# Expert-row combine: slots 0 to 3 fetched into four buffers and added at least two expert blocks later, slot 5 added by TensorE

## The chip, the cores and the metric

The kernel runs on one core of one Trainium2 chip. The metric is the device time of one execution in microseconds (us), lower is better. A core has TensorE (PE, matmuls into PSUM banks), VectorE (DVE), ScalarE (ACT), GpSimd (POOL) and SyncE (SP); SP, ACT and POOL also issue DMAs, which all run on the same 16 DMA engines.

## The reference

A transformer block of one kind (attention and a state-space branch, cross attention, then a mixture of experts) followed by one of another kind. The change touches the mixture of experts, its layer norm and the start of the second block:

```python
scores = sigmoid(x @ w_router)                 # 512 tokens, 64 experts, d = 1024
top_idx = 8 best experts of the 4 best groups of 8
w = scores[top_idx]; w = w / sum(w) * 2.5
for expert e: out_e = swiglu(x[tokens of e], w_exp_gu[e], w_exp_down[e])
routed[t] = sum over the 8 chosen experts of w * out_e[row of t]
ff = routed + swiglu(x, w_sh_gu, w_sh_down)    # the shared expert
x = layer_norm(2 ** 0.25 * x + ff, ln3_g, ln3_b)
h = rmsnorm(x); z = h @ w_in                   # the second block begins
```

Everything is float32.

## The kernel before, in words

The kernel is written as one program for each engine, with semaphores between them; nothing is scheduled automatically, so the order of each program is the order of the work.

**Expert blocks.** `e_block(u, b)` handles expert e = 4u + b on every engine, 64 of them. On PE a block turns the hidden rows of expert e-1 (L1240, `turn_hidden`), turns the gathered tokens of expert e+1 (L1233, `turn_rows`, which waits for that expert's gather), does the gate-up product of expert e (L1271) with the down product of expert e-2 woven in (L1279, L1289). PE waits for `ht_ready`, which DVE gives when it has copied the turned hidden rows (L2340, `hidden_turned`). ACT and DVE evacuate the results into `ye`, and ACT stores 96 rows per expert in `y_rows` (`y_send`, L1732; L1777 for the last two). POOL gathers the 96 token rows of expert e+1 or so from `x_rows` (L2716). SP loads 2 MB of gate-up and 1 MB of down weights per expert (L823, L826) into four slots: gate-up in `ring[:, 0:4096]`, `ring[:, 4096:8192]`, `slab1`, `slab2`.

**Slots.** The eight choices of a token are its slots 0 to 7, in the order of the experts' numbers. For slot k and token tile t (four tiles of 128 tokens) POOL gathers 128 rows of 4 KB from `y_rows` with an indirect DMA (`slot_rows(k, t)`, L2726), and the row is scaled by its weight and added to `acc`. Slot k can be fetched when expert 56 + k is stored (`slot_stored(k)`), since its row cannot belong to a later one. Slots 0 to 4 and 6 share the one buffer `work[:, 0:4096]`: tile t of slot k+1 is fetched when tile t of slot k has been added (semaphore `combined`). Slot 5 has `slab1`, slot 7 has `slab2`. DVE adds slots 0 to 6 (`combine(k, t)`, the L1926 instructions on `work,s5x,slab`, 128x1024): slots 0, 1, 2, 3 inside blocks 60, 61, 62, 63 between `y_rest` and the copy of the down results (L2384), slot 4 around the last two down products, then slots 5 and 6. PE adds slot 7 by a product of the diagonal matrix of its weights with the rows (`last_slot`, L1347), on top of the shared expert's down product (L1340) in the banks `sd`.

**After the slots.** For each tile DVE adds the `sd` banks and takes the moments (`slots_added`), POOL computes the root, DVE and ACT normalise, PE turns the result (`hT2`, L949) and begins the second block's first product, `uv` (L940). Its weights come as panels of `stream` in the ring buffer (L811); SP starts these loads once 24 adds are done (`combined` 24) and needs nothing else, since slots do not use the ring.

Of the kernel before, what the change touches and what calls it, by code (L numbers as in the profile page):

```python
# [27 lines left out]
ACT = mybir.ActivationFunctionType  # L28
# [496 lines left out]
def build(nc, a, out, scratch):  # L525

    plan = Plan(psum_order(), 8)
    with ExitStack() as ctx:
# [3 lines left out]
        def sem(name):  # L532
            return ctx.enter_context(nc.semaphore(name))
# [3 lines left out]
        def tile(name, i):  # L537
            return bank[plan.where[name, i]]
# [135 lines left out]
        diag = [work[:, 4096 + t * P:4096 + (t + 1) * P] for t in range(NT)]  # L674
        w_main, w_over, yrow_f = s5x[:, 3464:3496], s5x[:, 3496:3528], s5x[:, 3528:3560]
# [84 lines left out]
        ov = {n: sem("ov_" + n) for n in ("gather", "w", "store", "xtr", "xe", "gu", "silu", "hid", "ht", "htr", "dn", "yact", "ydve", "idx", "ygot", "added")}  # L760
        ygot = {k: [sem(f"ygot{k}_{t}") for t in range(NT)] for k in (0, 5, 7)}
        for k in (1, 2, 3, 4, 6):
            ygot[k] = ygot[0]
        diag_ready, acc_scaled = sem("diag_ready"), sem("acc_scaled")
# [30 lines left out]
        def _(sp):  # L795
# [102 lines left out]

            sp.wait_ge(combined, 24)
            for n in range(N1, len(PANELS)):  # L900
# [10 lines left out]
        def _(pe):  # L911
# [430 lines left out]

            def last_slot(t):
                pe.wait_ge(ygot[7][t], 16)
                pe.wait_ge(diag_ready, t + 1)
                for half in range(2):
                    mm = nc.tensor.matmul(tile("sd", 2 * t + half)[:, :], diag[t], yslot[7][t][:, half * 512:half * 512 + 512],  # L1347
                                          start=False, stop=True)
                    close(mm, "sd", 2 * t + half)
# [168 lines left out]
        def _(act):  # L1518
# [259 lines left out]
            act.wait_ge(w_ready, 1)  # L1778
            for t in range(NT):
                nc.scalar.activation(diag[t], ident, ACT.Copy, scale=w_main[:, 28 + t:29 + t]).then_inc(diag_ready, 1)  # L1780
            act.wait_ge(route_ctrl, 3)
# [26 lines left out]
            act.wait_ge(combined, 28)  # L1808
            act.dma_start(wsT, a["gmlp_ws"]).then_inc(in_ln, 16)
# [92 lines left out]
        def _(dve):  # L1902
# [452 lines left out]
            def combine(k, t):  # L2355
                dve.wait_ge(acc_scaled, t + 1)
                dve.wait_ge(ygot[k][t], 16 * {5: 1, 6: 6}.get(k, k + 1))
# [44 lines left out]
            for b in range(2):  # L2402
                combine(4, 2 * b)
                dve.wait_ge(y_stored[b], 16 * (NE // 2 - 1))
                y_full(b, 5 - 5 * b, dnf_full, b + 1, yf_dve)
                combine(4, 2 * b + 1)
            dve.wait_ge(combined, added[0])
# [42 lines left out]

            for t in range(NT):
                combine(5, t)
            dve.wait_ge(in_ln, 96)
# [178 lines left out]
        def _(pool):  # L2632
# [89 lines left out]

            def slot_rows(k, t, buf_free=None):
                if buf_free is not None:
                    pool.wait_ge(combined, buf_free)
                pool.indirect_dma_start(yslot[k][t], None, scratch["y"][0:CAP * PITCH, :],  # L2726
                                        bass.IndirectOffsetOnAxis(ap=yrow_i[:, 4 * k + t:4 * k + t + 1].bitcast(U32), axis=0),
                                        bounds_check=CAP * PITCH - 1, oob_is_err=False).then_inc(ygot[k][t], 16)

# [5 lines left out]
            for e in range(NE):  # L2735
# [7 lines left out]
                gather(e)  # L2743
            for k in range(1, 5):
                slot_stored(k)
                for t in range(NT):
                    slot_rows(k, t, 4 * (k - 1) + t + 1)
            n_ov = pool.value_load(ctrl_i[0:1, NOV:NOV + 1], min_val=0, max_val=NOV)
            with pool.If(n_ov > 0):
                pool.wait_ge(xtr_full, NE)  # L2750
                nc.gpsimd.tensor_copy(tiny[:, 4:5], minus_half[:, 0:1]).then_inc(ov["idx"], 1)
                with pool.Fori(0, NOV) as o:
                    with pool.If(n_ov > o):
                        pool.wait_ge(idx_ov, 16 * o + 16)
# [16 lines left out]
                pool.wait_ge(ov["added"], 4 * TOPK)  # L2771

            slot_stored(5)
            pool.wait_ge(gu_full, 3 * NE)
            for t in range(NT):
                slot_rows(5, t)
            pool.wait_ge(combined, 20)
# [72 lines left out]
```

## Time and profile before

| what | value |
|---|---|
| median of 3 runs | 2170.53 us (2170.22 to 2173.47) |
| the profiled execution | 2177.02 us, its span 2175.2 us |
| PE, DVE, ACT, POOL busy | 1979.7, 779.9, 465.7, 335.5 us |
| mean granted clock of PE | 0.972 of 2.4 GHz |
| expert blocks and slots | about 670 to 1366 us of the span |

The busy times are sums over the whole span; the times of instructions below are counted from the span's start. "Idle before" in a timeline row stands in square brackets with what ended it. A matmul of float32 counts as two instructions in the trace.

### The profile page before, as it was taken

The numbers are of one execution on the slowest core, as the hardware profiler recorded it, in microseconds if no ns is written. First come the engines' busy times: TensorE is split into PE (matmuls) and PEld (weight loads), VectorE is DVE, ScalarE is ACT, GpSimd is POOL, SyncE is SP. The second block draws the span as 40 slices with busy tenths as digits, with TensorE's granted clock in tenths as the row PEclk, the third lists the DMA queues.
The fourth block names the chain that finished last, engine by engine and source line by source line (L and its number), as shares of the span: only waits on it lengthen the run. The fifth ranks groups of instructions, "written<-read, shape, count | busy, mean of one in ns | idle before, by whom it ended". The sixth has DMA issues, their size and how long they took to land.

```text
span 2175.2 us, 25449 instructions
## 1 busy us (share of the span) xinstructions
PE 1979.7 (91%) x9890; PEld 909.8 (42%) x9890; DVE 779.9 (36%) x1577; ACT 465.7 (21%) x1023; POOL 335.5 (15%) x295
## 2 busy tenths in 40 slices
PE   7887999999997999998989857699989899999997
PEld 3334434445543344433333322345745444444443
DVE  5998781214266233323232326501375200000012
ACT  2234431110310233333333311210263000000000
POOL 0653260000025211011000014200032000000000
PEclk9898999999999999999999988799999999999999
DMA  5129934213235999999999986512310222222210
GB/s 227 48 65 205 213 96 163 77 49 119 97 139 188 342 398 402 402 398 387 387 380 389 387 337 224 206 68 86 117 40 1 77 77 77 77 77 77 69 38 29
DMA packets 74723, 393.59 MB, mean 181 GB/s; under 512 B 12194, under 2 KB 12450, under 8 KB 57760
## 3 DMA queue, kind: packets, MB, share of 16 engines
q1 hardware_dynamic: 45216, 300.95, 36.7%
q10 hardware_dynamic: 16592, 58.01, 9.6%
q0 software_dynamic: 12848, 33.74, 4.4%
q8 instruction: 42, 0.69, 0.1%
q14 instruction: 25, 0.20, 0.0%
HBM read 371.51 MB, written 55.09 MB: 196 GB/s over the span
## 4 chain that ended last, share of the span: by engine, by line
PE 69%; DMA 15%; DVE 8%; issue 5%; POOL 2%; ACT 1%; another core or an unknown queue 0%; SPq 0%; POOLq 0%; DVEq 0%; ACTq 0%
PE bank L940 42%; DMA slab<-w_exp_down 13%; PE bank L1271 12%; PE bank L1492 6%; PE bank L949 2%; DVE slab L1926 1%; PE bank L1289 1%; DVE work L1920 1%; DVE s5x L1923 1%; DVE slab L1923 1%; PE bank L1002 1%; POOL slot_table L2705 1%; DVE slab L1920 1%; PE bank L1079 1%; PE bank L1233 1%
## 5 line engine op out<-in xcount | busy, mean ns | idle before, releaser
L940 PE MATMUL bank<-slab,ring 128*128 128x512 f32 (+1 forms) x1488 | 631.1, 585 | 13.1 <-DMA ring<-stream 11.4
L940 PEld LDWEIGHTS bank<-slab,ring 128*128 128x128 f32 x1488 | 281.8, 190 | 357.3 <-issue 354.7
L1271 PE MATMUL bank<-ring,slab 128*32 128x512 f32 x1536 | 230.2, 602 | 41.0 <-issue 24.1
L1271 PE MATMUL bank<-slab 128*32 128x512 f32 x1536 | 230.5, 599 | 29.7 <-DMA ring<-w_exp_down 17.4
L940 PE MATMUL bank<-ring,slab 128*128 128x512 f32 (+1 forms) x608 | 251.1, 573 | 3.6 <-DVE slab L1923 1.8
L1279 PE MATMUL bank<-ring,slab 128*32 128x512 f32 x512 | 228.8, 599 | 0.0
L1923 DVE TENSOR_TENSOR slab<-bank,slab 96x256 f32<-96x256 f32 (+2 forms) x120 | 64.7, 540 | 438.5 <-PE bank L940 295.0
L2384 DVE COPY slab<-bank 32x512 f32<-32x512 f32 x124 | 80.9, 688 | 392.9 <-PE bank L1279 392.8
L1279 PE MATMUL bank<-slab 128*32 128x512 f32 x480 | 213.2, 597 | 0.0
L940 PEld LDWEIGHTS bank<-ring,slab 128*128 128x128 f32 x608 | 114.9, 190 | 136.3 <-issue 128.6
L2641 POOL TENSOR_TENSOR small<-small 128x1 f32<-128x1 f32 (+2 forms) x30 | 26.6, 889 | 907.1 <-DVE small L1920 907.1
L1492 PE MATMUL bank<-ring,slab 128*128 128x512 f32 x352 | 151.3, 592 | 0.8 <-DVE slab L1923 0.8
L1271 PEld LDWEIGHTS bank<-ring,slab 128*32 128x32 f32 x1536 | 72.7, 111 | 173.2 <-issue 173.2
L1271 PEld LDWEIGHTS bank<-slab 128*32 128x32 f32 x1536 | 70.3, 110 | 163.9 <-issue 154.6
L2716 POOL DMA_INDIRECT slab<-x_rows,s5x x64 | 61.5, 961 | 499.3 <-PE bank L1233 479.5
L1492 PEld LDWEIGHTS bank<-ring,slab 128*128 128x128 f32 x352 | 66.8, 190 | 85.3 <-issue 83.7
L1752 ACT ACTIVATE slab<-bank 32x512 f32<-32x512 f32 x124 | 66.6, 584 | 117.5 <-PE bank L1279 108.9
L1708 ACT ACTIVATE slab<-bank 128x384 f32<-128x384 f32 x128 | 55.8, 488 | 161.8 <-DVE slab L2351 144.8
L1898 ACT ACTIVATE slab<-bank 128x512 f32<-128x512 f32 x22 | 13.1, 597 | 281.8 <-PE bank L940 281.8
L949 PE MATMUL bank<-const_sb,work 128*128 128x128 f32 x304 | 48.1, 292 | 20.3 <-DVE work L1920 14.9
L1233 PE MATMUL bank<-const_sb,slab 96*128 96x96 f32 x512 | 53.9, 249 | 11.7 <-DMA slab<-x_rows,s5x 10.6
L1525 ACT ACTIVATE slab<-bank 128x512 f32<-128x512 f32 (+2 forms) x40 | 22.7, 574 | 180.0 <-PE bank L940 170.2
(281 smaller groups left out, 2095.7 us busy)
## 6 DMA issues: line engine op xcount, KB each, us to landing
ring<-stream SPq DMA_DIRECT2D x171, 512.0 KB, 3.5
slab<-w_exp_gu SPq DMA_DIRECT2D x32, 2048.0 KB
ring<-w_exp_gu SPq DMA_DIRECT2D x32, 2048.0 KB
ring<-w_exp_down SPq DMA_DIRECT2D x32, 1024.0 KB
slab<-w_exp_down SPq DMA_DIRECT2D x32, 1024.0 KB
y_rows<-zeros ACTq DMA_DIRECT2D x1, 24960.0 KB, 130.7
y_rows<-slab ACTq DMA_DIRECT2D x64, 384.0 KB
gb<-rows ACTq DMA_DIRECT2D x5, 512.0 KB, 5.3
```

The costliest lines, as they stand in the source:

```text
L940: mm = nc.tensor.matmul(dst, lhs[k], rhs[k], start=(k == 0), stop=(k == len(lhs) - 1))
L949: mm = nc.tensor.transpose(tile(name, i)[0:parts, j * P:(j + 1) * P], x, ident)
L1233: mm = nc.tensor.transpose(bank[j][:, k * CAP:(k + 1) * CAP], xg[b][0:CAP, (4 * j + k) * P:(4 * j + k + 1) * P], ident[0:CAP, 0:CAP])
L1271: mm = nc.tensor.matmul(g_bank[32 * g:32 * g + 32, :], x[:, k, 32 * g:32 * g + 32], w[:, 512 * k:512 * k + 512], start=(k == 0), stop=(k = ...
L1279: mm = nc.tensor.matmul(bank[2 + 3 * t + half][96:128, :], h[:, c * CAP + 32 * t:c * CAP + 32 * t + 32], d[:, c * D + 512 * half:c * D + 5 ...
L1492: return nc.tensor.matmul(tile("fd", 4 * half + t)[:, :], actf[k][:, t * P:(t + 1) * P], panel("fd", 11 * half + k // 2)[:, (k % 2) * 512: ...
L1708: i = nc.scalar.activation(xe[b][:, 4 * j:4 * j + 4, :], bank[j][:, 0:4 * CAP].rearrange("p (k n) -> p k n", n=CAP), ACT.Copy)
L1752: i = nc.scalar.activation(ye[b % 2][0:32, 512 * half:512 * half + 512], bank[2 + half][96:128, :], ACT.Copy)
L1920: return nc.vector.tensor_scalar(out_, in_, s1, s2, op0, op1)
L1923: return nc.vector.tensor_tensor(out_, x, y, op)
L2384: i = nc.vector.tensor_copy(ye[b % 2][32:64, 512 * half:512 * half + 512], bank[5 + half][96:128, :])
L2716: pool.indirect_dma_start(xg[e % 2][0:CAP, :], None, scratch["x2"], bass.IndirectOffsetOnAxis(ap=slot_tok[:, e:e + 1].bitcast(U32), axis=0 ...
```

## The change

Slots get homes: slot 0 and 4 in `work`, 1 and 7 in `ring[:, 0:4096]`, 2 in `ring[:, 4096:8192]`, 3 and 6 in `slab1`, 5 in `slab2`. POOL fetches slots 1 to 3 when the gate-up product that uses that buffer is over, no longer when the slot before has been added. DVE adds slot 0 in block 62, slot 1 in block 63, slot 2 around the last down products, slots 3 and 4 after them, then slot 6. Slot 5 is added by PE with a second set of diagonal matrices. A slot in `work`, `ring_hi` or `slab2` has one semaphore for its four tiles together. The panels of the second block are loaded when the last slot product is over.

```diff
-        yslot = {k: [x[:, t * D:(t + 1) * D] for t in range(NT)] for k, x in ((0, work), (5, slab1), (7, slab2))}
-        for k in (1, 2, 3, 4, 6):
-            yslot[k] = yslot[0]
+        SLOT_HOME = {0: "work", 1: "ring_lo", 2: "ring_hi", 3: "slab1", 4: "work", 5: "slab2", 6: "slab1", 7: "ring_lo"}
...
+        home_got = {h: [sem(f"{h}_got{t}") for t in range(NT if h in ("slab1", "ring_lo") else 1)] for h in homes}
+        def ygot(k, t):
+            g = home_got[SLOT_HOME[k]]
+            return g[t % len(g)], 16 * nth_use[k] * (NT // len(g))
...
-            sp.wait_ge(combined, 24)
+            sp.wait_ge(combined, 12)
+            sp.wait_ge(psum_full, plan.full("sd", 7))
             for n in range(N1, len(PANELS)):
                 load_panel(n)
...
+            def add_slot(k, t):
+                pe.wait_ge(*ygot(k, t))
+                pe.wait_ge(diag_ready, t + 1 + 4 * (k == 7))
                 for half in range(2):
+                    mm = nc.tensor.matmul(tile("sd", 2 * t + half)[:, :], diag[k][t], yslot[k][t][:, half * 512:half * 512 + 512],
+                                          start=False, stop=(k == 7))
...
             for t in range(3):
                 shared_down(t)
-            last_slot(0)
+            add_slot(5, 0)
+            add_slot(5, 1)
+            add_slot(7, 0)
             shared_down(3)
-            for t in range(1, NT):
-                last_slot(t)
+            add_slot(5, 2)
+            add_slot(7, 1)
+            add_slot(5, 3)
+            add_slot(7, 2)
+            add_slot(7, 3)
...
             for b in range(4):
-                e_block(NE // 4 - 1, b, first=1, slot_=b)
+                e_block(NE // 4 - 1, b, first=1, slot_=b - 2 if b >= 2 else None)
...
-                combine(4, 2 * b)
+                combine(2, 2 * b)
...
-            for t in range(NT):
-                combine(5, t)
+            for k in (3, 4):
+                for t in range(NT):
+                    combine(k, t)
...
-            for k in range(1, 5):
+            for k in range(1, 4):
                 slot_stored(k)
+                pool.wait_ge(gu_full, 3 * (NE - 4 + k))
                 for t in range(NT):
-                    slot_rows(k, t, 4 * (k - 1) + t + 1)
+                    slot_rows(k, t)
...
+            slot_stored(4)
+            pool.wait_ge(combined, 4)
+            for t in range(NT):
+                slot_rows(4, t)
             slot_stored(5)
             pool.wait_ge(gu_full, 3 * NE)
             for t in range(NT):
                 slot_rows(5, t)
-            pool.wait_ge(combined, 20)
             slot_stored(6)
             for t in range(NT):
+                pool.wait_ge(combined, 13 + t)
                 slot_rows(6, t)
                 if t == 0:
                     slot_stored(7)
```

On DVE, in the unrolled blocks 60 to 63, this is the order before from the hidden rows of block 60 on; the four SCALAR_TENSOR_TENSOR are `combine`.

```order
L2340 COPY slab<-bank 128x96 x2
L1923 TENSOR_TENSOR slab<-bank,slab 96x256
L2350 COPY slab<-bank 32x256
L2351 COPY slab<-bank 32x256
L1926 SCALAR_TENSOR_TENSOR slab<-work,s5x,slab 128x1024 x4
L2384 COPY slab<-bank 32x512 x2
L2340 COPY slab<-bank 128x96 x2
```

And this is the order now, from the last operation of block 61 to the first add of slot 1.

```order
L2397 COPY slab<-bank 32x512 x2
L2353 COPY slab<-bank 128x96 x2
L1936 TENSOR_TENSOR slab<-bank,slab 96x256
L2363 COPY slab<-bank 32x256
L2364 COPY slab<-bank 32x256
L1939 SCALAR_TENSOR_TENSOR slab<-work,s5x,slab 128x1024 x4
L2397 COPY slab<-bank 32x512 x2
L2353 COPY slab<-bank 128x96 x2
L1936 TENSOR_TENSOR slab<-bank,slab 96x256
L2363 COPY slab<-bank 32x256
L2364 COPY slab<-bank 32x256
L1939 SCALAR_TENSOR_TENSOR slab<-ring,s5x,slab 128x1024 x4
```

In blocks 60 and 61 no add stands any more between the copies that PE waits for; the first four stand in block 62.

On POOL, the gathers at the end of the expert blocks were in this order, the x_rows gather being that of expert 63.

```order
L2726 DMA work<-y_rows,yrow_i 128x1024 x4
L2716 DMA slab<-x_rows,s5x 96x1024
L2726 DMA work<-y_rows,yrow_i 128x1024 x16
```

Now they are in this order.

```order
L2738 DMA work<-y_rows,yrow_i 128x1024 x4
L2730 DMA slab<-x_rows,s5x 96x1024
L2738 DMA ring<-y_rows,yrow_i 128x1024 x8
L2738 DMA slab<-y_rows,yrow_i 128x1024 x4
```

The four gathers of slot 0 are still ahead of the gather of expert 63, and slots 1 to 3 go elsewhere behind it.

On PE, after the last down product, the shared product and the slot product stood so.

```order
L1340 MATMUL bank<-work,s5x 128x512 x12
L1347 MATMUL bank<-slab,work 128x512 x2
L1340 MATMUL bank<-work,s5x 128x512 x4
L1347 MATMUL bank<-slab,work 128x512 x6
```

Now slot 5 (the rows in `slab`) stands among them.

```order
L1346 MATMUL bank<-work,s5x 128x512 x12
L1353 MATMUL bank<-slab,s5x 128x512 x4
L1353 MATMUL bank<-ring,work 128x512 x2
L1346 MATMUL bank<-work,s5x 128x512 x4
L1353 MATMUL bank<-slab,s5x 128x512 x2
L1353 MATMUL bank<-ring,work 128x512 x2
L1353 MATMUL bank<-slab,s5x 128x512 x2
L1353 MATMUL bank<-ring,work 128x512 x4
```

Four matmuls of slot 5 are ahead of the first of slot 7, and eight in all are new.

## Rows read from the trace of the kernel before

**Rows 1.** Windows: busy us of each engine, PE's granted clock, DMA share, GB/s.

```profile
1200.00:1250.00 50.00, 44.68 (x452) 18.87 (x450) 15.06 (x38) 15.37 (x36) 4.78 (x5) 1.00 1.01 387
1280.00:1290.00 10.00, 0.00 (x0) 0.00 (x0) 1.81 (x2) 0.37 (x1) 1.00 (x1) 0.70 0.94 363
1290.00:1300.00 10.00, 0.00 (x0) 0.00 (x0) 4.11 (x5) 0.00 (x0) 2.01 (x3) 0.50 0.65 224
```

**Rows 2.** Timeline of PE: start us, us, instructions [idle before, what ended it].

```profile
1270.02 0.63 PE L1271 MATMUL bank<-ring,slab 128*32 128x512 f32 x3 [0.60 <-DMA slab<-w_exp_down]
...
1279.07 0.24 PE L1233 MATMUL bank<-const_sb,slab 96*128 96x96 f32 x1 [0.22 <-DMA slab<-w_exp_down]
1301.28 1.07 PE L1271 MATMUL bank<-ring,slab 128*32 128x512 f32 x3 [21.96 <-issue]
...
1310.91 0.82 PE L1233 MATMUL bank<-const_sb,slab 96*128 96x96 f32 x8
1312.04 0.63 PE L1271 MATMUL bank<-slab 128*32 128x512 f32 x3 [0.30 <-issue]
...
1319.91 0.39 PE L1240 MATMUL bank<-const_sb,slab 96*128 96x96 f32 x2
1326.24 1.07 PE L1271 MATMUL bank<-slab 128*32 128x512 f32 x3 [5.95 <-issue]
...
1336.82 0.39 PE L1240 MATMUL bank<-const_sb,slab 96*128 96x96 f32 x2
```

**Rows 3.** Timeline of DVE, blocks 60 and 61.

```profile
1283.40 1.28 DVE L1926 SCALAR_TENSOR_TENSOR slab<-work,s5x,slab 128x1024 f32<-128x1024 f32 x1 [12.72 <-DMA work<-y_rows,yrow_i]
...
1297.90 1.28 DVE L1926 SCALAR_TENSOR_TENSOR slab<-work,s5x,slab 128x1024 f32<-128x1024 f32 x1 [3.88 <-DMA work<-y_rows,yrow_i]
...
1300.55 0.42 DVE L2340 COPY slab<-bank 128x96 f32<-128x96 f32 x2
```

**Rows 4.** Timeline of POOL: gathers of slots (L2726) and of expert 63 (L2716).

```profile
1271.86 1.02 POOL L2726 DMA_INDIRECT work<-y_rows,yrow_i  x1 [10.70 <-DMA y_rows<-slab]
...
1277.08 0.98 POOL L2716 DMA_INDIRECT slab<-x_rows,s5x  x1 [0.30 <-issue]
1285.56 1.00 POOL L2726 DMA_INDIRECT work<-y_rows,yrow_i  x1 [7.50 <-DVE slab L1926]
...
1356.19 1.61 POOL L2726 DMA_INDIRECT slab<-y_rows,yrow_i  x1 [1.21 <-DMA y_rows<-slab]
...
1365.27 0.99 POOL L2726 DMA_INDIRECT slab<-y_rows,yrow_i  x1 [0.30 <-issue]
```

**Rows 5.** Timeline of ACT's queue: the last store of expert rows.

```profile
1350.42 0.32 ACTq L1777 DMA_DIRECT2D y_rows<-slab  x1
```

**Rows 6.** Timeline of PE from the shared product to the second block.

```profile
1351.76 12.26 PE L1340 MATMUL bank<-work,s5x 128*128 128x512 f32 x24 [2.23 <-issue]
1363.87 1.88 PE L1347 MATMUL bank<-slab,work 128*128 128x512 f32 x4
1365.58 3.60 PE L1340 MATMUL bank<-work,s5x 128*128 128x512 f32 x8
...
1380.64 3.78 PE L1347 MATMUL bank<-slab,work 128*128 128x512 f32 x4 [1.91 <-DMA slab<-y_rows,yrow_i]
1395.43 5.93 PE L949 MATMUL bank<-const_sb,slab 128*128 128x128 f32 x32 [11.00 <-ACT slab L1801]
```

**Rows 7.** Timeline of DVE: the first add of slot 5, then the tiles' sums.

```profile
1354.45 2.48 DVE L1926 SCALAR_TENSOR_TENSOR slab<-slab,s5x 128x1024 f32<-128x1024 f32 x2 [2.93 <-issue]
...
1364.99 1.48 DVE L1923 TENSOR_TENSOR slab<-bank,slab 128x512 f32<-128x512 f32 x2 [3.48 <-PE bank L1347]
...
1370.80 1.48 DVE L1923 TENSOR_TENSOR slab<-bank,slab 128x512 f32<-128x512 f32 x2 [0.19 <-PE bank L1347]
```

**Rows 8.** DMA issues from 1345 to 1420 us: KB each, median us to landing.

```profile
ring<-stream SPq DMA_DIRECT2D x12, 512.0 KB, 15.7
...
slab<-y_rows,yrow_i POOLq DMA_INDIRECT x8, 7.1
```

More of the change, by code:

```diff
@@ L670, in build @@
         dn_w = [ring[:, 8192:10240], ring[:, 10240:12288], slab3[:, 0:2048], slab3[:, 2048:4096]]
-        yslot = {k: [x[:, t * D:(t + 1) * D] for t in range(NT)] for k, x in ((0, work), (5, slab1), (7, slab2))}
-        for k in (1, 2, 3, 4, 6):
-            yslot[k] = yslot[0]
-        diag = [work[:, 4096 + t * P:4096 + (t + 1) * P] for t in range(NT)]
+        SLOT_HOME = {0: "work", 1: "ring_lo", 2: "ring_hi", 3: "slab1", 4: "work", 5: "slab2", 6: "slab1", 7: "ring_lo"}
+        homes = {"work": work[:, 0:4096], "ring_lo": ring[:, 0:4096], "ring_hi": ring[:, 4096:8192], "slab1": slab1[:, :], "slab2": slab2[:, :]}
+        yslot = {k: [homes[h][:, t * D:(t + 1) * D] for t in range(NT)] for k, h in SLOT_HOME.items()}
+        nth_use = {k: sum(SLOT_HOME[j] == h for j in range(k + 1)) for k, h in SLOT_HOME.items()}
+        diag = {5: [s5x[:, 2048 + t * P:2048 + (t + 1) * P] for t in range(NT)],
+                7: [work[:, 4096 + t * P:4096 + (t + 1) * P] for t in range(NT)]}
         w_main, w_over, yrow_f = s5x[:, 3464:3496], s5x[:, 3496:3528], s5x[:, 3528:3560]
@@ L760, in build @@
         ov = {n: sem("ov_" + n) for n in ("gather", "w", "store", "xtr", "xe", "gu", "silu", "hid", "ht", "htr", "dn", "yact", "ydve", "idx", "ygot", "added")}
-        ygot = {k: [sem(f"ygot{k}_{t}") for t in range(NT)] for k in (0, 5, 7)}
-        for k in (1, 2, 3, 4, 6):
-            ygot[k] = ygot[0]
+        home_got = {h: [sem(f"{h}_got{t}") for t in range(NT if h in ("slab1", "ring_lo") else 1)] for h in homes}
+        def ygot(k, t):
+            g = home_got[SLOT_HOME[k]]
+            return g[t % len(g)], 16 * nth_use[k] * (NT // len(g))
         diag_ready, acc_scaled = sem("diag_ready"), sem("acc_scaled")
@@ L1341, in shared_down @@
                                          sd_w[:, k * D + half * 512:k * D + half * 512 + 512], start=(k == 0), stop=False)
-            def last_slot(t):
-                pe.wait_ge(ygot[7][t], 16)
-                pe.wait_ge(diag_ready, t + 1)
+            def add_slot(k, t):
+                pe.wait_ge(*ygot(k, t))
+                pe.wait_ge(diag_ready, t + 1 + 4 * (k == 7))
                 for half in range(2):
-                    mm = nc.tensor.matmul(tile("sd", 2 * t + half)[:, :], diag[t], yslot[7][t][:, half * 512:half * 512 + 512],
-                                          start=False, stop=True)
-                    close(mm, "sd", 2 * t + half)
+                    mm = nc.tensor.matmul(tile("sd", 2 * t + half)[:, :], diag[k][t], yslot[k][t][:, half * 512:half * 512 + 512],
+                                          start=False, stop=(k == 7))
+                    if k == 7:
+                        close(mm, "sd", 2 * t + half)
             for t in range(3):
                 shared_down(t)
-            last_slot(0)
+            add_slot(5, 0)
+            add_slot(5, 1)
+            add_slot(7, 0)
             shared_down(3)
-            for t in range(1, NT):
-                last_slot(t)
+            add_slot(5, 2)
[3 more added lines that the diff above has]
+            add_slot(7, 3)
             for c in range(KD):
@@ L1778, in _ @@
             act.wait_ge(w_ready, 1)
-            for t in range(NT):
-                nc.scalar.activation(diag[t], ident, ACT.Copy, scale=w_main[:, 28 + t:29 + t]).then_inc(diag_ready, 1)
+            for k in (5, 7):
+                for t in range(NT):
+                    nc.scalar.activation(diag[k][t], ident, ACT.Copy, scale=w_main[:, 4 * k + t:4 * k + t + 1]).then_inc(diag_ready, 1)
             act.wait_ge(route_ctrl, 3)
@@ L1807, in _ @@
                 scaled(t)
-            act.wait_ge(combined, 28)
+            act.wait_ge(combined, 24)
             act.dma_start(wsT, a["gmlp_ws"]).then_inc(in_ln, 16)
@@ L2356, in combine @@
                 dve.wait_ge(acc_scaled, t + 1)
-                dve.wait_ge(ygot[k][t], 16 * {5: 1, 6: 6}.get(k, k + 1))
+                dve.wait_ge(*ygot(k, t))
                 if t in last_add:
@@ L2402, in _ @@
             for b in range(2):
-                combine(4, 2 * b)
+                combine(2, 2 * b)
                 dve.wait_ge(y_stored[b], 16 * (NE // 2 - 1))
                 y_full(b, 5 - 5 * b, dnf_full, b + 1, yf_dve)
-                combine(4, 2 * b + 1)
+                combine(2, 2 * b + 1)
             dve.wait_ge(combined, added[0])
@@ L2449, in ln3_scale @@
                 stt(tm(x3, t), tm(x3, t), r, gb[:, D:2 * D], ALU.mult, ALU.add).then_inc(x3_ready, 1)
-            for t in range(NT):
-                combine(5, t)
+            for k in (3, 4):
+                for t in range(NT):
+                    combine(k, t)
             dve.wait_ge(in_ln, 96)
@@ L2721, in _, with slot_rows @@
             pool.wait_ge(x2_stored, 16 * NT)
-            def slot_rows(k, t, buf_free=None):
-                if buf_free is not None:
-                    pool.wait_ge(combined, buf_free)
+            def slot_rows(k, t):
                 pool.indirect_dma_start(yslot[k][t], None, scratch["y"][0:CAP * PITCH, :],
                                         bass.IndirectOffsetOnAxis(ap=yrow_i[:, 4 * k + t:4 * k + t + 1].bitcast(U32), axis=0),
-                                        bounds_check=CAP * PITCH - 1, oob_is_err=False).then_inc(ygot[k][t], 16)
+                                        bounds_check=CAP * PITCH - 1, oob_is_err=False).then_inc(ygot(k, t)[0], 16)
             def slot_stored(k):
@@ L2764, in _ @@
                     pool.wait_ge(y_stored[b], 16 * NE // 2)
-                pool.wait_ge(combined, 20)
+                pool.wait_ge(combined, 12)
                 for j in range(4 * TOPK):
@@ L2771, in _ @@
                 pool.wait_ge(ov["added"], 4 * TOPK)
+            slot_stored(4)
+            pool.wait_ge(combined, 4)
+            for t in range(NT):
+                slot_rows(4, t)
             slot_stored(5)
@@ L2776, in _ @@
                 slot_rows(5, t)
-            pool.wait_ge(combined, 20)
             slot_stored(6)
             for t in range(NT):
+                pool.wait_ge(combined, 13 + t)
                 slot_rows(6, t)
```

## The prediction

> **What bounds the kernel now.** I read the windows of ten microseconds first. In the expert blocks (1200 to 1250) PE is busy 44.7 of 50 us and the DMA engines are full at 387 GB/s; then come twenty microseconds in which PE does nothing [rows 1]. The timeline of PE gives the edges: it has turned the tokens for block 61's successor at 1279.31 (1279.07 + 0.24), and the gate-up product of block 61 starts at 1301.28, after 21.96 us idle [rows 2]. The trace calls the releaser "issue", which names nobody. DVE's timeline names it: the copy of the turned hidden rows that PE waits for is at 1300.55, and ahead of it stand the four adds of slot 0, the first after 12.72 us of waiting for its gather, the last at 1297.90 after another wait for one [rows 3]. So the adds, in the program between copies that PE needs, pass DVE's wait for a DMA on to PE. A second such stop is 5.95 us ahead of block 63 [rows 2]. What is slow is the gather: POOL issued it at 1271.86 [rows 4] and the data came 11 to 26 us later, because the weights filled the DMA engines [rows 1]. After the blocks PE, DVE and POOL share a chain through the tiles: PE's slot product, DVE's sums, the root, the turn `hT2` at 1395.43 [rows 6, 7]. Whatever moves that turn moves the end: nothing behind it is edited.
>
> **The change part by part.**
>
> *Blocks 60 and 61.* DVE holds no add in them now, so block 61 starts on PE as block 60 did: 0.6 us after the turning [rows 2], at 1279.9 in place of 1301.3. From a block's first product to the end of its turning of tokens takes 9.3 us (1270.02 to 1279.31); less the turning (0.8, the row at 1310.91) block 61 is through at 1288.4.
>
> *A new wait in block 62.* There PE turns the tokens of expert 63, whose gather POOL issues at 1277.08, behind the four gathers of slot 0 [rows 4], exactly as before. When it lands no row says. The last of slot 0, next ahead in the same queue, landed by 1297.90 [rows 3]; before the change PE turned these rows at 1310.91 without a wait [rows 2]. The four gathers of slot 0 (0.52 MB each) came through 14.5 us apart in all (1283.40 to 1297.90), 4.8 a piece; the 0.39 MB of this one cost 3.6 more at that rate, or 1.0 at the 387 GB/s of the full engines: 1298.9 to 1301.5. I take 1300.5. Two stores of expert rows, held back by the stop before, are now made in this stretch: 0.79 MB at 387 GB/s, 2.0 us. So the tokens are there at 1302.5, PE is idle for some 14 us, and the product of block 62 starts a turning later (1.1, from 1310.91 to 1312.04) at 1303.6, not 1312.04: 8.4 us gained. The earlier fetches of slots 1 and 2 are behind it in POOL's queue and cost it nothing as long as that order holds; that is the weak point, taken up below. Behind PE at this wait stand the products of blocks 62 and 63, and the two copies ACT and DVE make from them; DVE adds slot 0 in that time, which hides its 5.1 us (4 x 1.28).
>
> *The rest of blocks 62 and 63.* PE comes out of an idle stretch at 1.2 GHz (granted clock 0.50 in the windows' row 1290 to 1300 [rows 1]). Block 62, which started warm, takes 8.26 us from 1312.04 to the end of the turned hidden rows at 1320.30; block 63, after 5.95 idle, 10.97; block 61, after 21.96 idle, 9.6 to its end at 1310.9. A cold start so costs 1.4 to 2.7, I take 2.1. Before, from block 62's start: 8.26 + 5.95 + 10.97 = 25.2. Now: 8.26 + 2.1, then 1.3 for the copies between two blocks (between 0.6, the gap at 1270, and 2), then 8.26: 19.9. Gained 5.3, in all 13.7 at the end of block 63. Slot 1, added by DVE in block 63, was fetched over thirty microseconds earlier. The down products behind, and with them the last store (1350.42 [rows 5]), move by the same 13.7, to 1336.7.
>
> *POOL.* The first gather of slot 7 followed that last store by 5.8 us (1356.19 [rows 4]), so it can go at 1342.5. Slot 6 now waits for the adds of slot 3. DVE starts those where it started slot 5: 1354.45 - 13.7 = 1340.8 [rows 7], the first is done at 1342.1, and POOL issues 0.9 later, as it did at 1285.56 after the add at 1283.40 [rows 3, 4]: 1343.0. The order is 6, 7, 6, 7, so slot 7's first is issued at 1344.3, and eight gathers at 1.3 us put the last at 1352.1. With a median of 7.1 us to landing [rows 8] slot 7 is there from 1351.4 to 1359.2.
>
> *PE's tail.* The shared product starts at 1351.76 - 13.7 = 1338.1 and takes 12.1 [rows 6], to 1350.2. Then two tiles of slot 5 come first. A tile is 4 instructions, 1.71 us by 1363.87 to 1365.58: 3.4, to 1353.6. That is where slot 7's first tile may start; it landed at 1351.4, so its fetch is hidden with 2.2 us to spare. DVE adds the bank 1.1 after (1363.87 to 1364.99 [rows 6, 7]): 1354.7 against 1364.99, 10.3 gained. For the second tile PE does slot 7 (1.7), the shared product (3.4; 3.60 with overlap), slot 5 (1.7): 1360.4, and DVE can add at 1361.5 against 1370.80: 9.3 gained. From there DVE sets the pace, 6 to 7 us a tile, and PE needs 3.4 a tile. So of 13.7 us 4.4 are given back to the eight added matmuls, and 9.3 reach `hT2`.
>
> *DVE's tail.* Four adds leave (slot 5), eight come (slots 3, 4). They end at 1340.8 + 8 x 1.26 = 1350.9, slot 6's first at 1352.2, 2.5 ahead of the 1354.7 at which PE lets it go on: hidden, and 2.5 us of cover is all there is.
>
> *The panels.* They were issued from 1360 on, and are now issued from 1368 (PE's last slot product: 1360.4 + 1.7 x 4 + wait). `uv` needs eight of them 7 us after `hT2`, so at 1393. 4.2 MB at 387 GB/s take 10.9: hidden by 14 us, and even with the 15.7 us to landing of a crowded queue [rows 8] the eighth issue at 1374 arrives at 1390. For slots 6 and 7 it is a gain: PE's waits for slot 7 (1.91 at 1380.64 [rows 6]) had the panels beside them. I count none of it, as DVE sets the pace.
>
> *A rule.* The POOL gather at 1356.19 took 1.61 in place of 0.99 and ended 0.87 after DVE's adds did (1354.45 + 2.48 [rows 4, 7]). The Trainium skill, "SBUF — State Buffer", section "SBUF: two separate sides", says that DVE with two SBUF inputs and a GpSimd operation that reads SBUF exclude each other for a whole instruction; that row agrees. By the row a gather pays for one add, and since an add (1.26) is as long as an issue, the sum above stands. If POOL never gets in between adds that follow without a gap, it is the second rival.
>
> **The rivals.**
>
> 1. *As worked out*: 9.3 us faster, 2161.2 (5 to 13 us with the bounds: landing 1298.9 to 1304, cold start 1.4 to 2.7, gap 0.6 to 2). 54 in 100.
> 2. *POOL locked out by eight adds in a row.* Slot 6's first gather, due at 1343.0, then ends only when the adds do, 1350.9 + 0.9 = 1351.8; slot 7's first is issued at 1352.1 and lands at 1359.2, 5.6 later than PE could use it. The second tile is worth 3.7: 2167. For it: the 1.61. Against: that gather paid for what was left of adds already running, no more. 13 in 100.
> 3. *The gather of expert 63 is not held up*: the engines finish its parts out of order with slot 0's. PE then is not cold, and block 62 starts at 1289.5; another 14 + 2 us, 2145. Against it speaks that the engines are full up to 1290 (363 GB/s [rows 1]). Half of it is as likely: 2153. 8 in 100 together.
> 4. *The engines are the bound, and the change only fills them earlier.* Slots 1 and 2 (4.2 MB), the last 1 MB of weights and two stores (0.8 MB) are put into the stretch in which expert 63's tokens are awaited. If they share the engines with it instead of standing behind, 6.0 MB at 387 GB/s delay it by 15.5 us, at the 224 GB/s of the window 1290 to 1300 by 27. Block 62 then starts 13.5 to 25 later than I say, and the kernel is 4 to 16 us slower: 2175 to 2186. It is slower than before from a delay of 11 us on. For it: the slow gather of slot 0 under weights shows that queues share. Against: slot 0's four came in turn. 12 in 100.
> 5. *No change*: the stop moves whole from block 61 to 62 (tokens at 1308) and the tail takes the rest; 2168 to 2172. 13 in 100.
>
> **How the numbers follow.** The terms are against the profiled execution (2177.0, which is 6.5 above the median, its span 2175.2); the difference is applied to the median, 2170.5 - 9.3 = 2161.2. What can be told from no change is about 0.2%, 4.3 us. Faster by more: case 1 nearly whole (52), case 3 (8), a part of 2 and 5 (10): 0.70. Within: the rest of 1, most of 2 and 5: 0.19. Slower: nearly all of case 4, 0.11. The range runs from 2153, the half of case 3, to 2170, the better half of case 5, and leaves out 5 below and some 15 above; case 1's own is 2157 to 2166.
>
> **What the profile will show.** Right: block 61's product at 1280 with about 0.6 us before it; one stop of PE of 12 to 15 us in block 62, at the turning of tokens, ended by the gather from `x_rows`; no add of slots 0 or 1 that waits on DVE; PE without a gap over 1 us from the shared product to the last slot product; DVE's first sum about 10 us earlier, `hT2` at 1386. The prediction is wrong if the stop in block 62 is over 18 us or under 8, if POOL's gathers of slots 6 and 7 are over 2 us apart, if DVE and not PE is late at the first tile, or if `uv` waits for panels.

## The result and the profile after

The changed kernel takes 2160.43 us (median of 4, 2160.15 to 2162.68) against 2171.48 us for the kernel before in the same comparison (median of 4): ratio 0.9951, 95% interval 0.9933 to 0.9968, so 3.2 to 6.7 thousandths faster. The forecast was 2161.2, in a range of 2153 to 2170. A second comparison gave 0.9946 (0.9927 to 0.9964).

The profiled execution takes 2160.7 us, its span 2158.8. That is 16.4 less than the span before, but 5.3 of it lie ahead of the change: block 60 starts its product at 1264.75, before it was at 1270.02 [rows 2]. Over the ten profiles below, whose programs have the same order of work up to there, block 60 starts anywhere from 1262.75 to 1273.31. So the profiles are compared from block 60's first product on.

The windows of the changed kernel (columns as in [rows 1]):

```profile
1200.00:1250.00 50.00, 45.01 (x461) 19.21 (x454) 14.52 (x35) 15.66 (x36) 4.78 (x5) 1.00 1.00 389
...
1280.00:1290.00 10.00, 2.19 (x30) 0.93 (x22) 2.90 (x7) 1.12 (x3) 3.60 (x5) 0.75 1.01 397
1290.00:1300.00 10.00, 2.08 (x12) 1.45 (x16) 4.87 (x4) 0.50 (x2) 0.80 (x1) 0.50 0.89 313
```

There is one stop of PE in these two windows now, in place of two windows without any work, and the DMA engines move 313 GB/s in the second, where they moved 224. The timeline of PE, to be held against [rows 2] and [rows 6]:

```profile
1264.75 0.63 PE L1277 MATMUL bank<-ring,slab 128*32 128x512 f32 x3 [0.60 <-DMA slab<-w_exp_down]
...
1273.94 0.63 PE L1277 MATMUL bank<-ring,slab 128*32 128x512 f32 x3 [0.28 <-DVE slab L2353]
...
1297.92 1.54 PE L1239 MATMUL bank<-const_sb,slab 96*128 96x96 f32 x8 [15.72 <-DMA slab<-x_rows,s5x]
1299.39 1.08 PE L1277 MATMUL bank<-slab 128*32 128x512 f32 x3
...
1309.88 0.63 PE L1277 MATMUL bank<-slab 128*32 128x512 f32 x3 [0.94 <-issue]
...
1319.31 0.35 PE L1246 MATMUL bank<-const_sb,slab 96*128 96x96 f32 x2 [1.17 <-DVE slab L1936]
1319.50 7.03 PE L1252 MATMUL bank<-slab 128*96 128x512 f32 x16
1328.74 12.26 PE L1346 MATMUL bank<-work,s5x 128*128 128x512 f32 x24 [2.21 <-issue]
...
1344.27 1.88 PE L1353 MATMUL bank<-ring,work 128*128 128x512 f32 x4
...
1376.38 5.73 PE L955 MATMUL bank<-const_sb,slab 128*128 128x128 f32 x32 [18.22 <-ACT slab L1814]
```

Block 61 starts after 0.28 us idle, not 21.96. Block 62 stops for 15.72 at the turning of tokens, and the row names the gather from `x_rows`. Then PE has no gap from the shared product to the last slot product. DVE's rows, against [rows 3] and [rows 7]:

```profile
1294.76 4.87 DVE L1939 SCALAR_TENSOR_TENSOR slab<-work,s5x,slab 128x1024 f32<-128x1024 f32 x4 [10.65 <-DMA work<-y_rows,yrow_i]
...
1345.40 1.48 DVE L1936 TENSOR_TENSOR slab<-bank,slab 128x512 f32<-128x512 f32 x2 [4.06 <-PE bank L1353]
...
1352.26 1.48 DVE L1936 TENSOR_TENSOR slab<-bank,slab 128x512 f32<-128x512 f32 x2 [1.24 <-PE bank L1353]
```

DVE still waits for slot 0's rows, but nothing that PE needs at that time stands behind. POOL's gathers, against [rows 4]:

```profile
1271.53 0.97 POOL L2730 DMA_INDIRECT slab<-x_rows,s5x  x1 [0.30 <-issue]
...
1334.15 2.02 POOL L2738 DMA_INDIRECT slab<-y_rows,yrow_i  x1 [0.30 <-DVE slab L1939]
1336.47 0.99 POOL L2738 DMA_INDIRECT ring<-y_rows,yrow_i  x1 [0.30 <-issue]
1337.77 2.02 POOL L2738 DMA_INDIRECT slab<-y_rows,yrow_i  x1 [0.30 <-issue]
...
1345.26 0.99 POOL L2738 DMA_INDIRECT ring<-y_rows,yrow_i  x1 [0.30 <-issue]
```

### The profile page after: what moved, and what is told of

It is laid out like the page before. It is cut to its first block, busy times and chain, and to the rows that moved or that the text cites. A ratio compares the mean times of both kernels' runs of the same rounds, so it can differ in the third digit from the quotient of the medians.

```text
span 2158.8 us, 25482 instructions
## 1 busy us (share of the span) xinstructions
PE 1982.0 (92%) x9906; PEld 914.1 (42%) x9906; DVE 774.4 (36%) x1573; ACT 467.1 (22%) x1027; POOL 337.5 (16%) x295
## 4 chain that ended last, share of the span: by engine, by line
PE 71%; DMA 13%; DVE 9%; issue 4%; POOL 2%; ACT 1%; POOLq 0%; SPq 0%; ACTq 0%; DVEq 0%
PE bank L946 42%; PE bank L1277 12%; DMA ring<-w_exp_down 9%; PE bank L1504 6%; PE bank L955 2%; DMA slab<-x_rows,s5x 2%; DVE slab L1939 2%; PE bank L1295 1%; DVE slab L1936 1%; DVE work L1933 1%; DMA slot_table<-tok_i,yrow_i 1%; DVE s5x L1936 1%; POOL slot_table L2719 1%; PE bank L1008 1%; DVE slab L1933 1%
## 5 line engine op out<-in xcount | busy, mean ns | idle before, releaser
L1277 PE MATMUL bank<-slab 128*32 128x512 f32 x1536 | 229.1, 600 | 22.2 <-DMA ring<-w_exp_down 15.7
```

Of the source, the lines that this page charges most:

```text
L1277: mm = nc.tensor.matmul(g_bank[32 * g:32 * g + 32, :], x[:, k, 32 * g:32 * g + 32], w[:, 512 * k:512 * k + 512], start=(k == 0), stop=(k = ...
```

## The experiments

Each ratio is to the kernel before in its own comparison. Two stages are taken from each profile: from block 60's first product to the turn `hT2`, and from there to the end of the span.

| kernel | median us | ratio (95%) | block 60 to turn | turn to end |
|---|---|---|---|---|
| before | 2171.48 | 1 | 125.4 (1270.02 to 1395.43) | 779.8 |
| changed | 2160.43 | 0.9951 (0.9933 to 0.9968) | 111.6 (1264.75 to 1376.38) | 782.4 |
| changed, again | 2160.71 | 0.9946 (0.9927 to 0.9964) | 112.5 (1262.75 to 1375.27) | 782.4 |
| adds early | 2188.02 | 1.0062 (1.0042 to 1.0082) | 134.5 (1269.45 to 1403.99) | 783.9 |
| one buffer, adds late | 2177.16 | 1.0010 (0.9998 to 1.0023) | 122.8 (1270.37 to 1393.19) | 784.1 |
| slot 5 by DVE | 2162.81 | 0.9945 (0.9925 to 0.9966) | 110.4 (1269.41 to 1379.78) | 782.5 |
| panels late | 2174.76 | 0.9997 (0.9983 to 1.0010) | 122.4 (1267.82 to 1390.17) | 780.0 |
| hold slots | 2164.92 | 0.9957 (0.9937 to 0.9977) | 113.0 (1273.31 to 1386.31) | 782.4 |
| gather first | 2158.09 | 0.9923 (0.9897 to 0.9949) | 108.2 (1263.86 to 1372.05) | 784.0 |
| gather first, adds later | 2152.62 | 0.9912 (0.9889 to 0.9934) | 101.9 (1266.31 to 1368.22) | 782.4 |

**Adds early: the buffers without the late adds.**

```diff
-                e_block(NE // 4 - 1, b, first=1, slot_=b - 2 if b >= 2 else None)
+                e_block(NE // 4 - 1, b, first=1, slot_=b)
...
-                combine(2, 2 * b)
+                combine(4, 2 * b)
...
-            for k in (3, 4):
-                for t in range(NT):
-                    combine(k, t)
```

> The buffers and slot 5 on PE as in the changed kernel, but DVE adds slots 0 to 3 in blocks 60 to 63 and slot 4 around the last down products, as before the change. Theory (the place of the adds is what frees PE): DVE again waits for slot 0's gather between copies that PE needs, PE idles some 20 us ahead of block 61, and only the shorter stop ahead of block 63 (5.95 us before) is gone; the kernel is within 5 us of the one before. Rival (the shared buffer, which let one slot wait for the next, was the cause): most of the 11 us stay, the time is near 2162.

It is 6.2 thousandths slower than the kernel before (2188.02 against 2174.18 us). The stop is back, and this run differs from the changed kernel only in the place of the adds, so their place was the cause. That the kernel would stay within 5 us of the one before was wrong, and so was that the stop ahead of block 63 would go. The timelines of PE, DVE and POOL of this run:

```profile
1304.52 1.08 PE L1277 MATMUL bank<-ring,slab 128*32 128x512 f32 x3 [25.80 <-issue]
...
1334.35 1.07 PE L1277 MATMUL bank<-slab 128*32 128x512 f32 x3 [10.36 <-issue]
```

```profile
1297.66 4.87 DVE L1939 SCALAR_TENSOR_TENSOR slab<-work,s5x,slab 128x1024 f32<-128x1024 f32 x4 [27.42 <-DMA work<-y_rows,yrow_i]
...
1327.44 4.90 DVE L1939 SCALAR_TENSOR_TENSOR slab<-ring,s5x,slab 128x1024 f32<-128x1024 f32 x4 [10.70 <-issue]
```

```profile
1314.57 0.98 POOL L2735 DMA_INDIRECT ring<-y_rows,yrow_i  x1 [28.99 <-PE bank L1277]
```

With one semaphore for four tiles DVE starts slot 0 when the last tile is there, so all four adds (4.87) stand behind it, where one did (1.28): 25.80 less 21.96 is 3.8 more, close to the 3.6 of three adds. And slot 2 may be fetched only when block 61's product is over, which stood in the stop itself: issued at 1314.57, waited for until 1327.44, and PE stops for 10.36 in place of 5.95. The buffer's release is a new wait, harmless only when the add is late.

**One buffer, adds late: the place without the buffers.** The kernel before, with

```diff
-                e_block(NE // 4 - 1, b, first=1, slot_=b)
+                e_block(NE // 4 - 1, b, first=1, slot_=b - 2 if b >= 2 else None)
...
-                combine(4, 2 * b)
+                combine(2, 2 * b)
...
-            for t in range(NT):
-                combine(5, t)
+            for k in (3, 4, 5):
+                for t in range(NT):
+                    combine(k, t)
```

and slot 4's fetch behind POOL's test for overflow.

> The kernel before, with its one shared buffer and slot 5 on DVE, but slot 0 added in block 62, slot 1 in block 63, slot 2 around the last down products, slots 3, 4, 5 and 6 after them. Theory (the place of the adds frees the blocks, the buffers free the tail): PE's only stop in the blocks is for expert 63's tokens as in the changed kernel, but slots 3 and 4 are each fetched only when the slot before is added, 6 to 9 us a slot, so the tail takes 10 to 15 us longer than in the changed kernel; the time is near the one before, 2168 to 2176. Rival (the buffers do nothing once the adds are late): within 3 us of the changed kernel.

As expected by the theory, the time is that of the kernel before within the interval (1.0010); at 2177.16 us it is just above the 2168 to 2176 that were named, with a kernel before at 2175.54 in that comparison. Its PE timeline has the new stop and then the missing buffers:

```profile
1302.03 1.54 PE L1233 MATMUL bank<-const_sb,slab 96*128 96x96 f32 x8 [12.38 <-DMA slab<-x_rows,s5x]
...
1360.01 3.78 PE L1347 MATMUL bank<-slab,work 128*128 128x512 f32 x4 [13.96 <-DMA slab<-y_rows,yrow_i]
```

Neither half gives anything alone in the time: 1.0062 and 1.0010, together 0.9951. The stages say where it goes. This kernel reaches the shared product 63.4 us after block 60's start (1270.37 to 1333.79), where the kernel before needs 81.7 (1270.02 to 1351.76): 18.3 us gained by the late adds. From there to the turn it needs 59.4 us (to 1393.19), before it was 43.7: the single buffer takes 15.7 of them back. The 2.6 us that are left at the turn go behind it, where nothing was edited (784.1 against 779.8, 4.3 lost); more on that below.

**Slot 5 by DVE: the change without its second half.** ACT makes only the diagonal matrices of slot 7.

```diff
-            for k in (3, 4):
+            for k in (3, 4, 5):
                 for t in range(NT):
                     combine(k, t)
...
-            add_slot(5, 0)
-            add_slot(5, 1)
             add_slot(7, 0)
             shared_down(3)
-            add_slot(5, 2)
             add_slot(7, 1)
-            add_slot(5, 3)
             add_slot(7, 2)
             add_slot(7, 3)
```

> The changed kernel, but DVE adds slot 5 after slots 3 and 4, and PE adds slot 7 alone. Theory (PE is ahead of the first tile's sum by two tiles of slot 5, and DVE had 4 us idle there): PE's first slot product of slot 7 is 3.4 us earlier if its rows are there, DVE has 5 us more of adds and becomes the one that is late, about 1 us later than now at the first sum, then DVE sets the pace: 0 to 2 us slower than the changed kernel, 2160 to 2163. Rival (the eight added products are what the tail costs): 3 to 4 us faster, near 2157.

The ratio is 0.9945 against 0.9951 and 0.9946: no difference that can be told. DVE's timeline shows the five adds without a gap and the first sum behind them, 17.98 us after the shared product (1332.41) where the changed kernel has 16.66 (1328.74 to 1345.40); the second tile's sum comes at 23.44 against 23.52.

```profile
1344.30 6.06 DVE L1935 SCALAR_TENSOR_TENSOR slab<-slab,s5x 128x1024 f32<-128x1024 f32 x5
...
1350.39 1.29 DVE L1932 TENSOR_TENSOR slab<-bank,slab 128x512 f32<-128x512 f32 x2
...
1355.85 1.29 DVE L1932 TENSOR_TENSOR slab<-bank,slab 128x512 f32<-128x512 f32 x2
```

So slot 5 on PE is neutral: it takes 5 us from DVE and gives PE 3.4 us ahead of the first tile, and from the second tile on both orders meet. Here the rival fell too, that the eight added products are what the tail costs: without them DVE is the one that is late.

**Panels late: the order of the panels' loads alone.** The kernel before, with

```diff
             sp.wait_ge(combined, 24)
+            sp.wait_ge(psum_full, plan.full("sd", 7))
```

> The kernel before, but the panels of the second block are loaded only when the last slot product is over, as in the changed kernel. Theory: PE's two waits for slot 7 (3.97 and 1.91 us) shrink, since the panels no longer load beside it, but DVE sets the pace there: 0 to 1 us faster than before; the product uv does not wait. Rival (late panels are what costs 2.6 us behind the turn in the changed kernel): uv or a later product waits for its panel, and 2 to 4 us are lost after the turn.

```profile
1338.98 7.03 PE L1247 MATMUL bank<-slab 128*96 128x512 f32 x16
...
1359.35 1.98 PE L1348 MATMUL bank<-slab,work 128*128 128x512 f32 x4 [0.58 <-DMA slab<-y_rows,yrow_i]
...
1366.86 1.98 PE L1348 MATMUL bank<-slab,work 128*128 128x512 f32 x4 [0.37 <-DMA slab<-y_rows,yrow_i]
1369.33 1.98 PE L1348 MATMUL bank<-slab,work 128*128 128x512 f32 x4 [0.49 <-DMA slab<-y_rows,yrow_i]
...
1390.17 2.18 PE L950 MATMUL bank<-const_sb,slab 128*128 128x128 f32 x9 [18.86 <-ACT slab L1802]
```

The waits for slot 7 shrink to half a microsecond, from 1.91 and more [rows 6], and `uv` waits for nothing (1.06 us after the turn). In the time it is not to be told from before (0.9997), though the stage up to the turn is 3.0 us shorter in this profile, 1.7 of it behind the start of the shared product (1348.20 to 1390.17 is 41.97, before 43.67). That is not shown to be the panels' doing, since PE's granted clock was higher in this profile. The 24 instructions of the shared product took 10.57 us here at a granted clock of 1.00, and 12.26 at 0.86 in the kernel before [rows 6]; the down products ahead of it took 7.03 here and 8.73 there, and PE's program is the same in both. The rival fell: from the turn to the end it needs 780.0, as before.

**Hold slots: does what stands behind in the queue cost the gather?**

```diff
+            pool.wait_ge(gathered[1], 16 * NE // 2)
             for k in range(1, 4):
                 slot_stored(k)
```

> The changed kernel, but POOL issues the gathers of slots 1 to 3 only when expert 63's tokens have landed. Theory (a queue is served in its order, so what stands behind costs the gather nothing): the tokens land within 1 us of the changed kernel's time from block 60's start (33.4 us), the time is 2160 within 2 us. Rival (the early fetches share the engines with it): the tokens land 2 to 6 us earlier and the kernel is faster by as much.

PE turns expert 63's tokens 24.8 us after POOL issued their gather (1280.50 to 1305.27). In the three profiles that let the fetches follow it is 26.4 and 27.0 in the changed kernel (1271.53 to 1297.92, and 1269.80 to 1296.78 in its second profile) and 25.6 in the run with slot 5 on DVE (1276.14 to 1301.72). So the fetches behind cost it 0.8 to 2.2 us of 26, and one profile each cannot say it closer. From block 60's start PE turns the tokens at 32.0 us, against 33.2, 34.0 and 32.3. That lies between the theory (within 1 us of 33.4) and the rival (2 to 6 us earlier), near the theory. The time (0.9957) is not to be told from the changed kernel's. What is left to make the gather late is what stands ahead of it, and the next run takes that away.

```profile
1280.50 0.98 POOL L2730 DMA_INDIRECT slab<-x_rows,s5x  x1 [0.30 <-issue]
```

```profile
1305.27 1.54 PE L1239 MATMUL bank<-const_sb,slab 96*128 96x96 f32 x8 [10.85 <-DMA slab<-x_rows,s5x]
```

**Gather first: the new wait taken away at its root.** The changed kernel, with expert 63's gather ahead of slot 0:

```diff
             for e in range(NE):
...
+                gather(e)
                 if e == NE - 1:
                     pool.wait_ge(route_ctrl, 3)
                     slot_stored(0)
                     for t in range(NT):
                         slot_rows(0, t)
-                gather(e)
```

> The changed kernel, with the gather of expert 63's tokens issued ahead of the four gathers of slot 0. Theory (that gather waits in its queue behind slot 0's 2.1 MB): it lands before block 61 ends, the 15.7 us stop in block 62 goes, and the next bound is the weights of block 63, which landed about 33 us after block 60's start: PE stops some 5 us ahead of block 63 in its place, and the kernel is 8 to 12 us faster than the changed one, near 2150. Rival (the DMA engines are full and any order ends at the same time): the stop moves whole to block 63 or the down products, and the time stays within 3 us of 2160.

Neither was right in full. The stop in block 62 is gone and block 62 starts at 20.8 us after block 60 in place of 34.6, as the theory has it; the time (2158.09, ratio 0.9923) is within the 3 us of 2160 that the rival gave, and its interval overlaps the changed kernel's. Of the 13.9 us only 3.4 are left at the turn (108.2 against 111.6), and 1.6 are lost behind it. PE and DVE of this run say where they went:

```profile
1284.62 0.63 PE L1277 MATMUL bank<-slab 128*32 128x512 f32 x3 [1.70 <-DMA ring<-w_exp_down]
...
1302.01 1.07 PE L1277 MATMUL bank<-slab 128*32 128x512 f32 x3 [9.14 <-DVE slab L2353]
```

```profile
1295.10 4.91 DVE L1939 SCALAR_TENSOR_TENSOR slab<-work,s5x,slab 128x1024 f32<-128x1024 f32 x4 [10.56 <-DMA work<-y_rows,yrow_i]
```

It is the fault of the kernel before, further on in the blocks: PE waits 9.14 us ahead of block 63 for a DVE copy that stands behind adds that wait for a gather.

**Gather first, adds later.** On top of that: slot 0 in block 63, slot 1 around the last down products, then slots 3, 2, 4, 6.

```diff
-                e_block(NE // 4 - 1, b, first=1, slot_=b - 2 if b >= 2 else None)
+                e_block(NE // 4 - 1, b, first=1, slot_=0 if b == 3 else None)
...
-                combine(2, 2 * b)
+                combine(1, 2 * b)
...
-            for k in (3, 4):
+            for k in (3, 2, 4):
...
-                pool.wait_ge(combined, 13 + t)
+                pool.wait_ge(combined, 9 + t)
                 slot_rows(6, t)
```

> Expert 63's tokens fetched ahead of slot 0, and the adds one block later still: slot 0 in block 63, slot 1 around the last down products, then slots 3, 2, 4 and 6. In the run with the gather first alone PE stopped 9.1 us ahead of block 63, because DVE stood at slot 0's adds until 1295.1 in block 62. Theory (an add that waits for a fetch hands its wait to PE wherever a copy stands behind it): that stop shrinks to 1 to 4 us, bounded by the weights of block 63, which land 31 us after block 60 starts; against the tail, which gets four more adds (5 us, of which 2.5 to 4 are hidden behind PE), the kernel is 2 to 5 us faster than with the gather first alone, 6 to 9 faster than the changed kernel in this call. Rival (the tail is the bound and takes it all): within 2 us of the run with the gather first.

2152.62 us, 8.1 less than the changed kernel in the same comparison (2160.71), where 6 to 9 were expected, and 0.9912 of the kernel before. PE's timeline:

```profile
1277.10 0.63 PE L1277 MATMUL bank<-ring,slab 128*32 128x512 f32 x3 [1.88 <-DMA slab<-w_exp_down]
1288.00 0.63 PE L1277 MATMUL bank<-slab 128*32 128x512 f32 x3 [1.99 <-DMA ring<-w_exp_down]
1298.80 0.63 PE L1277 MATMUL bank<-slab 128*32 128x512 f32 x3 [2.54 <-DMA ring<-w_exp_down]
```

Blocks 61, 62 and 63 follow each other 10.8 to 10.9 us apart, each after 1.9 to 2.5 us for its weights. What bounds these blocks is the DMA: the slots' fetches and the weights share the engines, whose share is 1.00, 1.01 and 1.01 from each start to the next (372, 418 and 402 GB/s).

**The changed kernel again.**

> The changed kernel again, as the yardstick of this call and for a second profile. Theory: 0.5% faster than before; from block 60's first product to the turn hT2 111 to 112 us as in its first profile, and 782 from there to the end of the span. Rival (the 2.6 us lost behind the turn were chance): 780 from the turn to the end, as in the kernel before.

112.5 and 782.4 us: the first stage within 1 us, and the 2.6 us behind the turn are there again. Its stop in block 62 is 16.58 us, with the tokens turned at 34.0.

## Why the prediction was right, step by step

*The cause of the stop* (adds that wait for a fetch, between copies that PE needs): shown from both sides, by the changed kernel (0.28 us idle) and by the adds put back (25.80).

*The new wait in block 62*: foreseen in place and kind. Tokens 32.5 us after block 60's start, measured 33.2 and 34.0 in the two profiles; idle 14, measured 15.72 and 16.58, just above the 12 to 15 that were named. The product of block 62 was to gain 8.4, and gained 7.4 (34.6 us after block 60's, before 42.0). That its length is the queue ahead, slot 0's 2.1 MB, is shown by the gather put first. Rival 4, that the earlier fetches share the engines with this gather and delay it by 15.5 us or more, fell: holding them back gained 0.8 to 2.2. Rival 3 (no wait at all) and rival 5 (the stop moves whole) fell with the same rows.

*From block 62 to the shared product*: the term that was mis-sized. I took 5.3 us; it is 10.4 (1299.39 to 1328.74 is 29.35, before 1312.04 to 1351.76 is 39.72). The 5.1 us between the two have three parts. The first, 1.2 us, lies in blocks 62 and 63: the cold start cost 1.3 (1299.39 to 1308.95 is 9.56, against 8.26) where I took 2.1, and the gap between the blocks was 0.94 where I took 1.3. The other two are prices that I carried over from the kernel before as they were:

```profile
1340.61 0.36 PE L1240 MATMUL bank<-const_sb,slab 96*128 96x96 f32 x2 [3.41 <-DVE slab L1923]
1340.81 8.73 PE L1246 MATMUL bank<-slab 128*96 128x512 f32 x16
```

The wait of 3.41 us for DVE ahead of the last hidden rows is 1.17 now. In it DVE's copy stood idle for 2.25 us, which the trace puts down to "remote" and to no engine of this core; the same is there in the run with late panels (1.92, PE's wait 3.08) and in no profile whose adds or buffers differ (PE waits 1.17 to 2.09 us there). What DVE waited for stays open. The down products take 7.03 us where they took 8.73, and that is PE's clock: the granted clock over these 16 instructions was 0.81 before (1340.6 to 1349.4) and is 1.00 now (1319.3 to 1326.6), and 0.81 of 8.80 us are 7.1. The change is not needed for it: with late panels, where PE has the old program and its stops of 22.87 and 6.14 us, they take 7.03 as well, and with the adds early, behind stops of 25.80 and 10.36 us, again 7.03. So I had taken a clock level of one execution for a constant. In all it is 17.8 us at the shared product, not 13.7, and 1.7 of them are that level.

*The tail gives back*: forecast 4.4 us, measured 4.0 (17.8 at the shared product, 13.8 at the turn; the first sum gains 14.3, the second 13.3). PE was late at the first tile as said: DVE idle 4.06 for PE, and 2.5 of cover was said. But the prediction put the loss down to the eight added matmuls, and that was only half the truth: with slot 5 on DVE the tail is as long, so it is the four more adds or the four more tiles of product, whichever engine gets them.

*POOL behind the adds*: two gathers took 2.02 in place of 0.99 and those between 0.99, so eight took 11.1 us from first to last issue against 9.1 worked out. Two of them started 2.32 us after the one ahead, which was named as a sign of a wrong prediction (over 2 us apart); it cost nothing, as slot 7 was there when PE asked: no wait at 1344.27. Rival 2, that POOL never gets in between adds, fell. The Trainium skill, "SBUF — State Buffer", section "SBUF: two separate sides", has a DVE operation with two SBUF inputs and a GpSimd operation that reads SBUF exclude each other for a whole instruction. The two rows of 2.02 fit that (1.03 more, less than an add); the rows of 0.99 at 1336.47 and 1340.09, under the same adds without a gap, show no such wait.

*The panels*: issued from 1358.27, 18 us ahead of the turn; `uv` came 1.2 us after the turn, without a wait for them.

*Behind the turn*: the prediction said that nothing is edited there and put the term at nothing. 2.6 us are lost, in both profiles of the changed kernel. The windows of three stretches, counted from the turn, show what differs; first the kernel before:

```profile
1575.43:1595.43 20.00, 16.28 (x79) 8.81 (x77) 14.64 (x56) 9.99 (x34) 3.34 (x2) 1.00 0.28 105
1660.43:1680.43 20.00, 17.96 (x100) 10.40 (x97) 4.45 (x10) 1.77 (x3) 1.60 (x2) 1.00 0.00 1
1695.43:1715.43 20.00, 13.68 (x53) 8.74 (x53) 8.27 (x14) 4.63 (x6) 1.28 (x1) 0.91 0.30 109
```

Then the changed kernel:

```profile
1556.38:1576.38 20.00, 16.67 (x77) 9.90 (x77) 13.99 (x53) 9.36 (x32) 3.33 (x2) 0.91 0.28 106
1641.38:1661.38 20.00, 17.96 (x108) 10.65 (x104) 3.70 (x9) 1.77 (x3) 1.27 (x2) 0.91 0.00 1
1676.38:1696.38 20.00, 13.68 (x52) 8.63 (x51) 8.27 (x14) 4.03 (x5) 1.28 (x1) 0.83 0.29 105
```

The mean granted clock is 1.00, 1.00, 0.91 before and 0.91, 0.91, 0.83 now, with the same work: a mean that is 0.08 to 0.09 lower over 20 us is 3.2 to 3.6 us at 1.2 instead of 2.4 GHz, so up to 1.8 us of lost work in each of the three. One product shows it bare, first before and then now:

```profile
1667.77 27.71 PE L940 MATMUL bank<-ring,slab 128*128 128x512 f32 x64
```

```profile
1649.46 29.41 PE L946 MATMUL bank<-ring,slab 128*128 128x512 f32 x64
```

The same 64 instructions take 1.7 us more. Over all ten profiles this product and the middle stretch go with the time behind the turn: a clock of 1.00 and 27.71 us where it is 779.8 and 780.0, 0.91 and 29.40 to 29.41 us in the eight where it is 782.4 to 784.1. (The first stretch does not sort them: it is at 0.91 with late panels too.) Two runs separate this from the parts of the change, by one profile each: late panels alone give 780.0, and the one-buffer kernel, which has early panels, no slot 5 on PE and the old buffers, gives 784.1. So the late panels do not bring the loss, and neither the buffers nor slot 5 on PE are needed for it. What decides whether the clock drops there, with pieces of work that are the same, stays open.

So the mechanism was right, and the forecast of 9.3 us came nearer to the 11.05 of the medians than its terms deserve, by luck: two errors offset, 13.8 gained up to the turn, not 9.3, and 2.6 lost behind it, not nothing.

## What to carry to other kernels

An operation that waits for a transfer, written between two that another engine needs, hands its wait on; look in the waiting engine's program for what stands behind. When it is moved, ask two things of the trace: what is the next transfer the freed engine will meet, and what is ahead of it in its queue. Before a duration of a product is carried over as a price, read the granted clock beside it: the same 16 down products took 8.73 us at 0.81 and 7.03 at 1.00, without any edit between. And test the halves apart: here separate buffers alone made the kernel slower, and late adds alone left its time as it was.

## What had not been expected of the hardware

The four gathers of a slot, 0.52 MB each, landed 5.5 to 7.4 us after their issue in the changed kernel's slots 3 to 7 (medians of each four), nearly all issued in windows where the DMA engines were busy for 0.85 to 0.91 of the time (1310 to 1350). The slots issued while weights were still loading (0, 1 and 2, a share of 0.89 to 1.02) had medians of 14 to 28 us. In the kernel before, with the panels' loads beside them, slots 6 and 7 had 12.4 and 11.1. Holding back everything behind expert 63's gather shortened its wait by 0.8 to 2.2 us of 26; putting it ahead of slot 0's four took the stop away. The work behind the turn is the same in all ten profiles, yet eight of them need 782.4 to 784.1 us for it, the kernel before 779.8 and the one with late panels 780.0; in the eight the granted clock is lower in the same stretch.
